# A one-input copy in place of a product with ones on GpSimd, in a hybrid attention step on one core

## The chip, the cores and the metric

The kernel runs on one NeuronCore of a Trainium2 chip. The metric is the device time of one execution in microseconds. A NeuronCore has a matrix engine (TensorE, PE in the profile; PEld is its weight load), VectorE (DVE), ScalarE (ACT), GpSimd (POOL) and SyncE (SP), which here only issues DMAs. They run their own instruction lists and wait for each other by semaphores.

## The reference

Two layers of a streaming encoder are applied to 1024 frames of a new stream and 64 frames of a running one; both share all weights. Everything is float32.

```python
# even layer: x -> x + y @ w_out
h = rmsnorm(x); z = h @ w_in                    # 1024 -> 5648 columns
aq, ak, av, bq, bk, bv, blr, gate = split(z)
ao = sliding_window_attention(aq, ak, av)       # 16 heads of 64, 4 KV heads, chunks of 64, sinks, ALiBi
bo = rmsnorm(gla(bq, bk, bv, log_sigmoid(blr @ w_lr + b_lr) / 16))   # 4 heads, 128 x 256 state
y = concat(ao, bo) * silu(gate)
# odd layer: x -> x + y @ w_out
xb, gate = split(rmsnorm(x) @ w_in)             # 1024 -> 2 x 1536
u = causal_conv4(xb)                            # width 4, per channel
rg, ig = sigmoid(blockdiag(u, w_ra)), sigmoid(blockdiag(u, w_ri))
a = exp(-8 rg softplus(-lam)); b = sqrt(1 - a*a) * ig * u
h_t = a_t * h_(t-1) + b_t                       # a scan over time
y = h * silu(gate)
# at the end: rmsnorm of x; keys, values and states are returned too
```

## The kernel before, in words

Activations lie transposed in the on-chip memory, features on the 128 partitions and 1092 columns of time, taken in 3 chunks of 364. Every weight matrix is cut into pieces of 128 x 1024 numbers, 113 of them, in the order in which they are used. A float32 product is made of three matmuls in the shorter format float32r: the weight W is split into w_hi (W rounded to float32r) and w_lo = W - w_hi, the activation likewise into H_hi and H_lo, and PE adds w_hi*H_hi + w_lo*H_hi + w_hi*H_lo.

The weight's path has four engines. SP loads piece p into `raw[:, p % 2]`, once `w_split` says that both halves of piece p - 2 are split (L326). GpSimd splits it in two halves of 512 columns: `w_hi` (L349), then `w_lo` (L353), in the slot p % 2 of each. Before it overwrites a half of `w_hi` it waits until PE is through with that half of the piece two before (`half_done` for the first half, `piece_done` for the second, L348). PE waits for `w_split` before the first matmul that reads a half (L382, L427), so at any time one piece is being multiplied and the next is split. SP's and GpSimd's loops run over pairs of pieces; the first two pieces, which wait for nothing of PE's, and the last one stand outside GpSimd's loop.

The stages, by the trace's time: the norm of x and the first pieces (0 to about 60 us); keys and values; attention (about 104 to 485 us), in which the matmuls of the next group of heads (L562) lie between scores (L494), transposes (L510) and products with the values (L522); the gated linear attention, four heads (to about 840); its output projection and the second layer's norm (to about 1050); the second layer's four groups (to about 1440); its output projection and the final norm.

VectorE's instructions that the prediction speaks of: L1171 makes H_lo at the start, L1236 copies a group's last values before attention starts on it, L1296 scales the probabilities, L1594 and L1598 are the first and the three further steps of the convolution, L1605 the low part of u, L1611 to L1616 the input term of the scan, L1619 and L1621 the scan for both streams, L1624 takes the gate's projection out of PSUM, which lets PE have that PSUM set again, and L1570 makes the low part of y. In the second layer's groups these run one behind the other on one engine for each of three 128-channel blocks, and PE waits for `drained`, `u_lo_done` or `y_lo_done` when it has no other work left. `ones` is a 128 x 128 tile of ones, also used by PE to sum over partitions.

Of the kernel before, what the change touches and what calls it, by code (L numbers as in the profile page):

```python
# [26 lines left out]
ALU = mybir.AluOpType  # L27
# [4 lines left out]
P = 128  # L32
# [29 lines left out]
PIECES = PC_OO + 2 * KD + 1  # L62
HALF = PIECE // 2
# [59 lines left out]
def tail_cols(c):  # L123
    a, b = TAIL[c]
    return slice(a * P, min(b * P, LIVE))
# [15 lines left out]
def build_program(nc, xT, weights, vecs_d, consts_d, wlr_d, kc_d, vc_d, sg_d,  # L141
# [5 lines left out]
    with ctx:  # L147
        at_byte = [32 * -(-nc.sbuf_base // 32)]

        def sb(name, shape, dt=F32, at=None):  # L150

            size = 4 * int(np.prod(shape[1:]))
            if at is None:
                at = at_byte[0]
                at_byte[0] += 32 * -(-size // 32)
            return nc.alloc_sbuf_tensor_at(name, shape, dt, offset=at)

        def sem(name):
            return ctx.enter_context(nc.semaphore(name))
# [7 lines left out]
        raw = sb("raw", [P, 2, PIECE])  # L167
        w_hi = sb("w_hi", [P, 2, PIECE], F32R)
# [3 lines left out]
        ones = sb("ones", [P, P])[:, :]  # L172
# [104 lines left out]
        ones_set, w_hi_done, w_split = sem("ones_set"), sem("w_hi_done"), sem("w_split")  # L277
# [40 lines left out]
        @block.sync  # L318
        def _(sp):
            sp.dma_start(raw[:, 0, :], weights[0]).then_inc(w_in[0], 16)  # L320
            sp.dma_start(X[:, 0, :], xT[0]).then_inc(x_in[0], 16)
            sp.dma_start(raw[:, 1, :], weights[1]).then_inc(w_in[1], 16)
            with sp.Fori(1, PIECES // 2 - 2) as i:
                for s in range(2):
                    sp.wait_ge(w_split, 4 * i + 2 * (s - 1))
                    sp.dma_start(raw[:, s, :], one(weights, 2 * i + s)).then_inc(w_in[s], 16)  # L326
            for piece in range(PIECES - 4, PIECES - 1):
                sp.wait_ge(w_split, 2 * piece - 2)
                sp.dma_start(raw[:, piece % 2, :], weights[last_pieces(piece)]).then_inc(w_in[piece % 2], 16)
            for c in range(3):  # L330
                cols = tail_cols(c)
                for b0, b1 in ((0, TAIL_POOL), (TAIL_POOL, 6), (6, KD)):
                    if b0:
                        sp.wait_ge(xn_done, (KD - TAIL_POOL) * c + b1 - TAIL_POOL)
                    else:
                        sp.wait_ge(xp_done, TAIL_POOL * (c + 1))
                    sp.dma_start(yT[b0:b1, :, cols].rearrange("b p n -> p b n"), X[:, b0:b1, cols])\
                      .then_inc(y_saved, 16)


        @block.gpsimd
        def _(pool):
            def split(i, s, first):
                pool.wait_ge(w_in[s], 16 * i + 16)
                for h in range(2):
                    cols = slice(h * HALF, (h + 1) * HALF)
                    if not first:
                        pool.wait_ge((half_done, piece_done)[h], 2 * i + (s - 1))  # L348
                    pool.tensor_tensor(w_hi[:, s, cols].rearrange("p (k n) -> p k n", n=P),  # L349
                                       raw[:, s, cols].rearrange("p (k n) -> p k n", n=P), every_tile_ones,  # L350
                                       ALU.mult).then_inc(w_hi_done, 1)
                    pool.wait_ge(w_hi_done, 4 * i + (2 * s + h + 1))
                    pool.tensor_tensor(w_lo[:, s, cols], raw[:, s, cols], w_hi[:, s, cols].bitcast(F32),  # L353
                                       ALU.subtract).then_inc(w_split, 1)

            every_tile_ones = ones.rearrange("p (k n) -> p k n", k=1).to_broadcast([P, HALF // P, P])
            pool.memset(ones, 1.0).then_inc(ones_set, 1)
            pool.wait_ge(ones_set, 1)
            for s in range(2):
                split(0, s, True)  # L360
            with pool.Fori(1, PIECES // 2 - 1) as i:
                for s in range(2):
                    split(i, s, False)
            split(PIECES // 2 - 1, 0, False)
            for c in range(3):
                cols = tail_cols(c)
                for b in range(TAIL_POOL):
                    if c == 0:
                        pool.wait_ge(weighted, b + 1)
                    if b == 0:  # L370
                        pool.wait_ge(fb_done, c + 1)
                    pool.tensor_tensor(X[:, b, cols], X[:, b, cols], fb[:, cols], ALU.mult).then_inc(xp_done, 1)
# [3 lines left out]
        def _(pe):  # L376
# [127 lines left out]
            def transposes(u, U):  # L504
                t, _ = unit(u)
                pe.wait_ge(pt_free, U + 1)
                pe.wait_ge(p_done, U + 1)
                for kt, _, rows in key_tiles(t):
                    for j in range(2):
                        mm = pe.transpose(ps[0:rows, 5 + u % 2, (2 * kt + j) * P:(2 * kt + j + 1) * P],  # L510
                                          Ssb[:, u % 3, j, kt * P:kt * P + rows], ident)
                mm.then_inc(pt_done, 1)
# [1304 lines left out]
```

## Time and profile before

| | |
|---|---|
| median of 3 runs | 1598.69 us (1594.52 to 1599.26) |
| the profiled execution | 1598.26 us |
| its span, first to last instruction | 1596.2 us |
| mean granted clock of PE | 0.983 |
| busy: PE / DVE / ACT / POOL | 1523.5 / 927.8 / 456.1 / 689.6 us |
| POOL, products w_hi (L349) | 226, 333.1 us in sum |
| POOL, differences w_lo (L353) | 226, 349.5 us in sum |

The busy time of an engine is the sum of its instructions' times; an instruction that has started and is held up by another engine counts as busy, so a longer time can hold a wait. The granted clock is the share of TensorE's full clock of 2.4 GHz that it was given; 0.5 stands for 1.2 GHz. In the lists of waits, "PE ps L388 <- DVE Y L1624" reads: PE's matmuls of L388 sat idle until VectorE's instruction of L1624 had finished. Times in the order of time are microseconds from the span's start.

### The profile page before, as it was taken

To read this page: it belongs to the slowest core of one execution; us is meant where nothing else is said; L and a number is where in the kernel's file an instruction comes from. 1 tells how busy PE (TensorE), PEld (TensorE's weight loads), DVE (VectorE), ACT (ScalarE), POOL (GpSimd) and SP (SyncE) were. 2 spreads that over 40 slices of the span, in tenths; PEclk is the share of its full clock that TensorE was granted. 3 is DMA by queue.
4 is the path that set the end of the run, shared out by engine and by line. 5 is a ranking of instruction groups with operands and counts; after the bars stand their busy time and mean duration, and the time that the engine had idled before them with its cause. 6 is when DMAs were issued, how large, how long until landed. Compare 5 with 4: busy or idle time off the path is not lost.

```text
span 1596.2 us, 24860 instructions
## 1 busy us (share of the span) xinstructions
PE 1523.5 (95%) x9622; PEld 1432.1 (90%) x9622; DVE 927.8 (58%) x1423; ACT 456.1 (29%) x808; POOL 689.6 (43%) x466
## 2 busy tenths in 40 slices
PE   6998999999989999999999999989999999989997
PEld 5997777777769999999999999989999999989996
DVE  7114867777775454744459111378887878985113
ACT  5111423333353222122133000225335143362001
POOL 5252212222212333523435444556666565656553
PEclk9999999999999999999999999999999999999998
DMA  4210010100000111110112332111111111113223
GB/s 181 89 60 27 27 42 16 39 26 29 27 29 32 34 32 45 40 34 30 34 44 68 104 101 95 54 55 53 53 40 53 53 40 54 53 53 106 86 81 112
DMA packets 29330, 89.16 MB, mean 56 GB/s; under 512 B 3600, under 2 KB 8784, under 8 KB 29264
## 3 DMA queue, kind: packets, MB, share of 16 engines
q1 hardware_dynamic: 19632, 64.27, 12.1%
q10 hardware_dynamic: 9632, 23.91, 4.6%
q8 instruction: 53, 0.87, 0.2%
q14 instruction: 13, 0.11, 0.0%
HBM read 76.64 MB, written 11.67 MB: 55 GB/s over the span
## 4 chain that ended last, share of the span: by engine, by line
PE 56%; DVE 8%; issue 4%; POOL 2%; ACT 2%; ACTq 0%; POOLq 0%; DVEq 0%
PE ps L388 41%; PE ps L433 6%; POOL w_hi L349 1%; DVE Y L1598 1%; PE ps L707 1%; PE ps L562 1%; POOL w_lo L353 1%; PE ps L628 1%; PE ps L612 1%; PE ps L623 1%; DVE arena L1616 1%; DVE Yr L1383 1%; DVE arena L1613 1%; DVE arena L1621 1%; DVE arena L1619 1%
## 5 line engine op out<-in xcount | busy, mean ns | idle before, releaser
L349 POOL TENSOR_TENSOR w_hi<-raw,ones 128x512 fp32r<-128x512 f32 x226 | 333.1, 1474 | 864.1 <-PE ps L388 484.1
L388 PE MATMUL ps<-H,w_hi 128*128 128x364 f32 x2796 | 568.6, 331 | 23.3 <-DVE H L1171 15.2
L388 PEld LDWEIGHTS ps<-H,w_hi 128*128 128x128 f32 x2796 | 479.5, 189 | 27.0 <-issue 16.4
L388 PE MATMUL ps<-H,w_lo 128*128 128x364 f32 x1716 | 379.6, 330 | 0.0
L353 POOL TENSOR_TENSOR w_lo<-raw,w_hi 128x512 fp32r<-128x512 f32 x226 | 349.5, 1547 | 17.7
L388 PEld LDWEIGHTS ps<-H,w_lo 128*128 128x128 f32 x1716 | 300.2, 189 | 0.0
L562 PE MATMUL ps<-H,w_hi 128*128 128x364 f32 x672 | 148.0, 347 | 0.0
L388 PE MATMUL ps<-Yr,w_hi 128*128 128x364 f32 x636 | 140.7, 329 | 0.0
L907 ACT ACTIVATE arena<-arena,sm 128x256 f32<-128x256 f32 (+1 forms) x144 | 69.6, 484 | 225.3 <-DVE sm L1282 225.3
L433 PE MATMUL ps<-w_hi,H 128*128 128x256 f32 (+1 forms) x720 | 132.4, 284 | 1.6 <-POOL w_lo L353 1.0
L1520 DVE TENSOR_TENSOR arena<-ps,arena 128x1092 f32 (+1 forms) x15 | 19.4, 1295 | 195.3 <-PE ps L388 195.3
L562 PEld LDWEIGHTS ps<-H,w_hi 128*128 128x128 f32 x672 | 115.5, 194 | 11.2 <-issue 10.5
L433 PEld LDWEIGHTS ps<-w_hi,H 128*128 128x128 f32 (+1 forms) x720 | 110.0, 185 | 3.1 <-POOL w_lo L353 1.8
L388 PEld LDWEIGHTS ps<-Yr,w_hi 128*128 128x128 f32 x636 | 110.8, 189 | 0.0
L433 PE MATMUL ps<-w_lo,H 128*128 128x256 f32 (+1 forms) x360 | 101.5, 282 | 0.0
L1082 ACT ACTIVATE arena<-arena 128x1092 f32<-128x1092 f32 x15 | 16.8, 1118 | 258.7 <-DVE arena L1520 253.6
L1270 DVE SCALAR_TENSOR_TENSOR arena<-consts,cur_sink,ps 128x256 f32<-128x256 f32 (+1 forms) x144 | 59.4, 453 | 51.6 <-PE ps L494 50.6
L388 PE MATMUL ps<-ur,w_hi 128*128 128x364 f32 x336 | 72.1, 342 | 13.2 <-DVE Y L1624 8.3
L562 PE MATMUL ps<-H,w_lo 128*128 128x364 f32 x336 | 78.5, 343 | 0.0
L388 PEld LDWEIGHTS ps<-ur,w_hi 128*128 128x128 f32 x336 | 59.8, 197 | 15.7 <-DVE Y L1624 10.6
L433 PEld LDWEIGHTS ps<-w_lo,H 128*128 128x128 f32 (+1 forms) x360 | 66.5, 185 | 0.3
L1598 DVE SCALAR_TENSOR_TENSOR Y<-arena,cur,Y 128x1092 f32<-128x1092 f32 x36 | 65.9, 1830 | 1.3
(202 smaller groups left out, 1894.0 us busy)
## 6 DMA issues: line engine op xcount, KB each, us to landing
raw<-weights SPq DMA_DIRECT2D x113, 512.0 KB, 3.3
arena<-xT ACTq DMA_DIRECT2D x15, 546.0 KB, 5.0
x_scratch<-arena ACTq DMA_DIRECT2D x8, 546.0 KB, 5.3
arena<-x_scratch ACTq DMA_DIRECT2D x8, 546.0 KB, 3.6
arena<-k_scratch ACTq DMA_DIRECT2D x8, 304.0 KB, 4.3
yT<-arena SPq DMA_DIRECT2D x2, 768.0 KB, 4.4
yT<-arena SPq DMA_DIRECT2D x2, 576.0 KB, 3.3
k_scratch<-Y ACTq DMA_DIRECT2D x2, 512.0 KB, 2.7
```

Of the source, the lines that this page charges most:

```text
L349: pool.tensor_tensor(w_hi[:, s, cols].rearrange("p (k n) -> p k n", n=P), raw[:, s, cols].rearrange("p (k n) -> p k n", n=P), every_tile_ones,
L353: pool.tensor_tensor(w_lo[:, s, cols], raw[:, s, cols], w_hi[:, s, cols].bitcast(F32), ALU.subtract).then_inc(w_split, 1)
L388: mm = pe.matmul(sets[st][:, c, 0:CW], lw[:, s, w], rx[:, k, c * CW:(c + 1) * CW], start=(first and n == 0 and m == 0), stop=(last and n = ...
L433: mm = pe.matmul(ps[0:m, 6 + t % 2, 0:256], lx[:, k, t * P:t * P + m], rw[:, s, wk], start=(k == 0 and n == 0), stop=(k == KD - 1 and n == 2))
L562: mm = pe.matmul(sets[0][:, c, 0:CW], lw[:, 1 - n % 2, k * P:(k + 1) * P], rx[:, k, c * CW:(c + 1) * CW], start=(x == 0), stop=(x == 3 * K ...
L612: pe.matmul(ps[:, 6 + t % 2, 0:256], kdT[0:r, t % 2, :], Vb[0:r, t, :], start=True, stop=True).then_inc(gds_done, 1)
L623: pe.matmul(ps[:, 3 + t % 2, e * P:e * P + r], Vb[0:r, t, cols], aT[0:r, t % 2, 0:r], start=True, stop=False)
L907: act.activation(Ssb[0:r, r3, j, c0:c1], Ssb[0:r, r3, j, c0:c1], ACT.Exp, bias=sm[0:r, r3, 2 + j:3 + j], scale=float(A_DIM) ** -0.5, accum ...
L1082: act.activation(sq, X[:, b, :], ACT.Square).then_inc(sq_done, 1)
L1270: last = dve.scalar_tensor_tensor(Ssb[0:r, r3, j, c0:c1], dist[0:r, c0:c1], cur_sink[0:r, 2, 2 * b + j:2 * b + j + 1], ps[0:r, 3 + j, c0:c ...
L1520: dve.tensor_tensor(chunks(slot(X, 2 * i + s)), setv(s), chunks(res[:, s, :]), ALU.add)\
L1598: dve.scalar_tensor_tensor(U[:, n, :], xc[:, j:j + TOK], cur[:, n, j:j + 1], U[:, n, :], ALU.mult, ALU.add).then_inc(cv_step if j < 3 else ...
```

## The change

Two things are changed in GpSimd's program. The high part is made by a copy from `raw` to `w_hi`, which converts float32 to float32r, in place of a product of `raw` with the tile of ones repeated along the free dimension. And the loop over pairs of pieces is written out, so that every wait compares with a constant; the waits themselves, their counts and the order of the pieces stay.

```diff
-                    pool.tensor_tensor(w_hi[:, s, cols].rearrange("p (k n) -> p k n", n=P),
-                                       raw[:, s, cols].rearrange("p (k n) -> p k n", n=P), every_tile_ones,
-                                       ALU.mult).then_inc(w_hi_done, 1)
+                    pool.tensor_copy(w_hi[:, s, cols], raw[:, s, cols]).then_inc(w_hi_done, 1)
                     pool.wait_ge(w_hi_done, 4 * i + (2 * s + h + 1))
                     pool.tensor_tensor(w_lo[:, s, cols], raw[:, s, cols], w_hi[:, s, cols].bitcast(F32),
                                        ALU.subtract).then_inc(w_split, 1)
 
-            every_tile_ones = ones.rearrange("p (k n) -> p k n", k=1).to_broadcast([P, HALF // P, P])
+
             pool.memset(ones, 1.0).then_inc(ones_set, 1)
             pool.wait_ge(ones_set, 1)
-            for s in range(2):
-                split(0, s, True)
-            with pool.Fori(1, PIECES // 2 - 1) as i:
-                for s in range(2):
-                    split(i, s, False)
-            split(PIECES // 2 - 1, 0, False)
+            for piece in range(PIECES - 1):
+                split(piece // 2, piece % 2, piece < 2)
```

On GpSimd, at the start of its program, before (ISA is an instruction without operands that the profile shows; here it is the pool's configuration, MODIFY_POOL_CONFIG):

```order
L357 MEMSET ones 128x128
L349 ISA
L349 TENSOR_TENSOR w_hi<-raw,ones 128x512 [waits w_in0,ones_set]
L353 TENSOR_TENSOR w_lo<-raw,w_hi 128x512 [waits w_hi_done]
L349 TENSOR_TENSOR w_hi<-raw,ones 128x512
L353 TENSOR_TENSOR w_lo<-raw,w_hi 128x512 [waits w_hi_done]
```

and the same place now, where w_lo's line has become L351:

```order
L355 MEMSET ones 128x128
L349 CAST w_hi<-raw 128x512 [waits w_in0,ones_set]
L351 ISA
L351 TENSOR_TENSOR w_lo<-raw,w_hi 128x512 [waits w_hi_done]
L349 CAST w_hi<-raw 128x512
L351 TENSOR_TENSOR w_lo<-raw,w_hi 128x512 [waits w_hi_done]
```

The configuration has moved from before the first operation on the weights to behind the first copy.

On GpSimd, the body of the loop before:

```order
L348 ISA [waits w_in0]
L349 TENSOR_TENSOR w_hi<-raw,ones 128x512 [waits half_done]
L352 ISA
L353 TENSOR_TENSOR w_lo<-raw,w_hi 128x512 [waits w_hi_done]
L349 TENSOR_TENSOR w_hi<-raw,ones 128x512 [waits piece_done]
L352 REGISTER_ALU
L353 TENSOR_TENSOR w_lo<-raw,w_hi 128x512 [waits w_hi_done]
L349 TENSOR_TENSOR w_hi<-raw,ones 128x512 [waits half_done,w_in1]
L352 REGISTER_ALU
L353 TENSOR_TENSOR w_lo<-raw,w_hi 128x512 [waits w_hi_done]
```

and the same pieces written out, which repeats to the end of the program:

```order
L349 CAST w_hi<-raw 128x512 [waits half_done,w_in0]
L351 TENSOR_TENSOR w_lo<-raw,w_hi 128x512 [waits w_hi_done]
L349 CAST w_hi<-raw 128x512 [waits piece_done]
L351 TENSOR_TENSOR w_lo<-raw,w_hi 128x512 [waits w_hi_done]
L349 CAST w_hi<-raw 128x512 [waits half_done,w_in1]
L351 TENSOR_TENSOR w_lo<-raw,w_hi 128x512 [waits w_hi_done]
```

The order of the operations on the weights is the same; the instructions that computed the counts to wait for are gone. GpSimd's program has 467 rows in place of 44. No other engine's instructions change.

## Rows read from the trace of the kernel before

**Rows 1.** The page, part 1: busy us (share of span) xinstructions.
```profile
PE 1523.5 (95%) x9622; PEld 1432.1 (90%) x9622; DVE 927.8 (58%) x1423; ACT 456.1 (29%) x808; POOL 689.6 (43%) x466
```

**Rows 2.** Stages: us, busy (x) per engine, granted clock, DMA, GB/s.
```profile
0.00:60.00 60.00, 44.81 (x244) 42.63 (x245) 32.26 (x26) 22.99 (x24) 29.84 (x24) 0.94 0.37 138
104.00:485.00 381.00, 355.78 (x2363) 290.57 (x2362) 264.58 (x780) 128.97 (x455) 87.86 (x68) 0.97 0.10 30
485.00:840.00 355.00, 352.43 (x2389) 336.54 (x2388) 183.74 (x234) 91.80 (x127) 129.00 (x88) 1.00 0.11 36
1050.00:1440.00 390.00, 372.14 (x2180) 367.90 (x2179) 321.39 (x278) 152.50 (x134) 237.97 (x140) 0.98 0.16 50
1194.00:1204.00 10.00, 7.61 (x37) 7.31 (x36) 7.24 (x8) 2.23 (x3) 4.85 (x4) 0.83 0.15 54
```

**Rows 3.** Waits of TensorE: engine line <- releaser: us, times, longest.
```profile
PE ps L388 <- DVE H L1171: 15.2, 4, 9.4
...
PE ps L510 <- DVE arena L1296: 11.0, 11, 1.7
...
PE ps L494 <- DVE arena L1236: 10.0, 4, 2.9
...
PE ps L388 <- DVE Y L1624: 8.3, 7, 2.4
...
PE ps L388 <- issue: 5.5, 2, 4.8
...
PE ps L388 <- DVE Yr L1570: 4.3, 1, 4.3
...
PE ps L433 <- POOL w_lo L353: 1.0, 4, 0.3
```

**Rows 4.** GpSimd's groups by form: busy us, mean ns | idle before.
```profile
L353 POOL TENSOR_TENSOR w_lo<-raw,w_hi 128x512 fp32r<-128x512 f32 x226 | 349.5, 1547 | 17.7
...
L349 POOL TENSOR_TENSOR w_hi<-raw,ones 128x512 fp32r<-128x512 f32 x226 | 333.1, 1474 | 864.1 <-PE ps L388 484.1 <-PE ps L562 254.6 <-PE ps L433 122.1
...
L372 POOL TENSOR_TENSOR arena<-arena 128x192 f32<-128x192 f32 x3 | 1.7, 590 | 1.8 <-ACT arena L1056 1.8
...
L357 POOL MEMSET ones<- 128x128 f32 x1 | 0.2, 205 | 0.3 <-POOLq L1800 0.3
...
L1800 POOL MEMSET const-float32-1.0<- 128x1 f32 x1 | 0.1, 99 | 0.0
```

**Rows 5.** By source line: duration ns min/median/max, first and last start.
```profile
L349 POOL TENSOR_TENSOR w_hi<-raw,ones x226: 1262/1295/2912, 4.3 to 1560.9; 128x512 fp32r<-128x512 f32 x113
...
L349 POOLq MODIFY_POOL_CONFIG  x2: 12/12/12, 0.9 to 0.9; - x2
...
L1594 DVE TENSOR_SCALAR Y<-arena,cur x12: 847/1764/1769, 1055.2 to 1369.4; 128x1092 f32<-128x1092 f32 x12
...
L1619 DVE TENSOR_TENSOR_SCAN arena<-arena x12: 2291/3266/3270, 1096.9 to 1425.7; 128x1024 f32<-128x1024 f32 x12
```

**Rows 6.** Order of time around 1175 to 1198 us: start us, us, what.
```profile
1175.96 1.38 POOL L349 TENSOR_TENSOR w_hi<-raw,ones 128x512 fp32r<-128x512 f32 x1 [0.36 <-PE ps L388]
...
1179.61 2.33 POOL L349 TENSOR_TENSOR w_hi<-raw,ones 128x512 fp32r<-128x512 f32 x1
...
1190.85 2.19 POOL L349 TENSOR_TENSOR w_hi<-raw,ones 128x512 fp32r<-128x512 f32 x1 [2.67 <-PE ps L388]
...
1176.23 6.88 DVE L1598 SCALAR_TENSOR_TENSOR Y<-arena,cur,Y 128x1092 f32<-128x1092 f32 x3
...
1191.92 3.27 DVE L1619 TENSOR_TENSOR_SCAN arena<-arena 128x1024 f32<-128x1024 f32 x1
...
1197.64 1.28 PE L388 MATMUL ps<-ur,w_hi 128*128 128x364 f32 x3 [2.39 <-DVE Y L1624]
```

**Rows 7.** Order of time, start of the program.
```profile
10.37 2.34 POOL L349 TENSOR_TENSOR w_hi<-raw,ones 128x512 fp32r<-128x512 f32 x1
...
11.50 2.37 DVE L1171 SCALAR_TENSOR_TENSOR H<-arena,vecs,H 128x1092 fp32r<-128x1092 f32 x1
```

## The prediction

> **What bounds the kernel now.** I read the page's busy shares first, then the stages, then who TensorE waits for, then GpSimd's own groups, and last the order of time at the places where TensorE stands still. TensorE is busy 1523.5 of 1596.2 us [rows 1]; the reader is to see that no other engine comes near, so only what fills or widens its 72.7 us of gaps can move the end, with what its clock loses around them. GpSimd, the engine that is changed, is busy 43% and sits idle 864.1 us in front of its high-part products, waiting for TensorE to free a weight slot [rows 1, 4]. Hence the change can't pay by GpSimd's throughput. The stages show where the gaps lie: 15.2 us in the first 60 us, 25.2 us in the attention stage (104 to 485), 2.6 us in the gated linear attention (485 to 840), 17.9 us in the second layer's groups (1050 to 1440) [rows 2]. The waits name their releasers: nearly all are VectorE instructions, and GpSimd itself is waited for in 1.0 us only [rows 3].
>
> So the question is what GpSimd does to VectorE. The rows of one instruction at its shortest and its median answer it: the bias of the convolution (L1594) takes 0.85 us at its shortest and 1.76 us in the median, the long scan (L1619) 2.29 and 3.27 us [rows 5]. In the order of time, each long one has a GpSimd operation running across its start: the scan begins at 1191.92 and a high-part product, issued at 1190.85, ends at 1193.04; the three convolution steps from 1176.23 to 1183.11 last 6.88 us while products run from 1175.96 and from 1179.61 [rows 6]. At the start of the program the product of 10.37 ends at 12.71, and VectorE's split of x, issued at 11.50, takes 2.37 us [rows 7]. The two engines take turns: a VectorE instruction that comes second is longer by about 0.9 to 1.0 us, and the GpSimd operation that comes second is longer too (1.26 us at its shortest, 1.47 in the mean, up to 2.91) [rows 4, 5].
>
> The Trainium skill says the same (SBUF — State Buffer, "Who interferes with whom"): the second port pair is one exclusive lock for the whole instruction, and whoever comes second blocks until the other ends. The trace agrees, with 2.29 against 3.27 us for the scan.
>
> **The change part by part.** *The copy.* It replaces 226 products that take 1.26 us undisturbed [rows 5]. No row shows a copy on GpSimd, so its time is bounded. Below: writing alone costs (205 - 99) ns over 127 elements, 0.83 ns each, plus 0.1 us [rows 4]; 512 elements give 0.53 us. On the other side of that: the two-input operation costs (1262 - 590) ns over 320 elements, 2.1 ns each [rows 4, 5], so a copy whose conversion costs as much as a second input is worth 1.26 us, and one that costs twice that slope besides 0.2 us is 2.4 us, the far end. I take 0.55 us, near the row of the writer with one stream, since the removed stream is the second read. The saving is then 0.7 us per operation.
>
> The Trainium skill (GPSIMD Engine Reference, "Engine selection") puts one-input operations at roughly line rate, by which the copy would be an estimated 0.5 to 0.6 us. The same page ("Elementwise — side-by-side cycle accounting") has 1.8 cycles per element as the best case of a tight loop, by which it would be an estimated 0.8 to 0.9 us and the sum below a little over half as large; no row here decides between the two.
>
> 226 times 0.7 us is 158 us of GpSimd's time, of which 864.1 us of idle [rows 4] hides all but what VectorE or TensorE waits for. I counted, in the order of time, the products that lie across VectorE's chain in front of a TensorE wait:
> - Start: two products, at 10.37 [rows 7] and 14.96, each between VectorE instructions that gate TensorE's first tiles: 2 x 0.7 = 1.4 us of the 15.2 [rows 3].
> - Attention: the four entries of a group wait 10.0 us for the small copies of L1236 [rows 3]; a product and then a difference precede them, and the copy before them bounds the gain to 0.5 us each: 2.0 us. Of the eleven waits on L1296, four or so have a product in the softmax's small steps, 0.6 us each: 2.4 us of 11.0.
> - Gated linear attention: the 1.0 us in which TensorE waits for the low parts [rows 3] goes: 1.0 us.
> - Second layer: four products before the wait of 4.8 us at 1072.7 (listed as issue), three before each of the two waits of 2.4 us (L1624), four before the one of 4.3 us (L1570) [rows 3, 6]: 14 x 0.7 = 9.8 us.
> - Clock: after the 2.39 us wait at 1197.64 [rows 6] the ten microseconds from 1194 have a granted clock of 0.83 [rows 2], so a third of them, 3.4 us, is at 1.2 GHz and costs 1.7 us. Where the wait shrinks to 0.3 us I expect no fall: two places, 3.4 us.
>
> Sum: 1.4 + 2.0 + 2.4 + 1.0 + 9.8 + 3.4 = 20.0 us. I take two thirds, 13 us, because the turns shift: a shorter copy lets the difference after it start earlier, at times across a VectorE instruction that was free before, and part of each chain belongs to ScalarE, which the change leaves alone.
>
> *The loop.* Written out, the program has no register or branch instructions between operations. On a chain of GpSimd this could only count if GpSimd were late; the next operation starts 0.1 us after the last in the looped part as well (1.38 us from 1175.96, the next at 1177.42). I cost it at nothing. If the fetch of some 460 instructions in place of 44 stalled, the 864.1 us of idle would cover it except in the 1.0 us of low-part waits.
>
> *The moved library instruction.* The pool configuration (0.9 us into the run, 12 ns by itself) stood before the first product, behind which GpSimd waited for the first weights anyway until 4.30 [rows 5]. Now it stands behind the first copy, so whatever it starts is in front of the first difference. That is 0 to 3.4 us (the length of the cover it had), and since TensorE's first wait lasts until 9.4 [rows 3] and the first low part would be ready at about 6.2 (4.30 + 0.55 + 1.26 and the step between them), the cover left is 3.2 us: nothing. Nor do SP's loads move; they wait for the same counts.
>
> The profiled execution took 1598.26 us (its span and 2.1 us around it), the median is 1598.69; the forecast is 1598.7 - 13, rounded to 1586 us.
>
> **The rivals.** *The copy is no shorter than the product* (1.2 to 1.4 us, or its conversion takes the time that the second read took). For it speaks that the cost per element of the product may be a software loop and not the port; against it the memset's 0.83 ns. Then nothing moves: 1597 to 1600 us.
>
> *The copy is shorter but VectorE's turns don't shorten*, because the difference, which comes right behind and is unchanged at 1.29 us, slides into the freed place. For it: between two VectorE instructions only one GpSimd operation fits, and there are as many as before. Against it: the products named above are separate turns. It leaves the 1.0 us of low-part waits and the start, 2 to 4 us: 1595 to 1597 us.
>
> *The copy is longer than the product*, and this is the slower case: a conversion loop that reads one stream but costs more per element. It decides from about 1.7 us on. The place is the same 28 turns (2 at the start, 8 in attention, 4 where the low parts are waited for, 14 in the second layer); at 2.4 us it adds 1.15 us to each, 32 us, by the same two thirds 21: 1620 us; at 1.8 us it is 10 us: 1609. Nothing in the trace excludes it, as no one-input arithmetic of this engine is in it; the memset speaks against it.
>
> *The copy at a middle price*, halfway between 0.53 and 1.26: 0.9 us saves 0.37 us a turn, so about half of 13: 1592 us. It belongs to the faster case, at its edge. The best-case loop of the page on GPSIMD in the Trainium skill (GPSIMD Engine Reference) would come out there.
>
> **How the numbers follow.** A measurement of this kernel tells about 0.3% (4.8 us) from no change. The copy at 0.5 to 1.0 us with its effect on the chains: 57%, 1578 to 1593 us, and 1586 as its value. Shorter but without effect: 10%. As long as the product: 13%. Longer: 20%. Faster by over 0.3% takes the first and a little of the second, 0.60; within 0.3% the rest of the middle ones, 0.18; slower 0.22, the last and a fetch or placement that goes wrong. The range runs from 1576 (the 20.0 us in full, and a little more clock) to 1609, where the copy of 1.8 us ends; about one in ten lies above it and somewhat less below.
>
> **What would show it.** The copy's row tells first: 0.5 to 0.9 us each is my case, over 1.5 us the slower one. Then the median of L1594 and L1619 should fall by 0.3 to 0.7 us, the waits on L1624 shrink from 2.4 to under 1 us and that on L1570 from 4.3 to about 2, the granted clock between 1194 and 1204 return to 1, and the waits for the low part vanish. VectorE's 927.8 us busy should fall by some 50 us. I am wrong if the copy is short and these waits stay, or if TensorE's first matmul moves behind 9.43 us.

## The result, and the profile after

The changed kernel takes 1561.36 us in the median (1556.69 to 1564.16, 4 runs) against 1598.97 us of the kernel before (1594.52 to 1600.82); the ratio is 0.9767, 95% interval [0.9745, 0.979]. It was timed once more beside other kernels: 1561.88 us against 1593.38, ratio 0.9793 [0.9766, 0.982]. So the gain is 2.1 to 2.3%, 31 to 38 us, where 13 were forecast; 1561 lies below the range of 1576 to 1609, and also below 1579, where the forecast's sum would have led without its discount.

The busy shares of the changed kernel, answering to [rows 1]; its span is 1554.8 us:

```profile
PE 1506.1 (97%) x9622; PEld 1419.1 (91%) x9622; DVE 850.3 (55%) x1423; ACT 455.9 (29%) x808; POOL 514.3 (33%) x466
```

TensorE is busy 17 us less for the same 9622 matmuls and idle 48.7 us in place of 72.7; VectorE is busy 77 us less with the same 1423 instructions.

Stage by stage, cut at the same matmuls in both traces: the start, attention, the gated linear attention, the second layer's groups. The columns are the stretch, its length, busy time (and instructions) of PE, PEld, DVE, ACT, POOL, then the granted clock, DMA share and GB/s. Before:

```profile
0.00:59.50 59.50, 44.31 (x240) 42.13 (x241) 32.00 (x25) 22.99 (x24) 29.62 (x23) 0.94 0.37 139
137.70:476.50 338.80, 316.45 (x2119) 251.54 (x2119) 252.62 (x760) 125.17 (x449) 72.41 (x56) 0.97 0.10 29
476.50:840.80 364.30, 360.94 (x2447) 345.05 (x2447) 190.10 (x248) 94.43 (x132) 129.66 (x88) 1.00 0.11 36
1045.10:1434.50 389.40, 371.68 (x2184) 367.57 (x2184) 318.74 (x277) 147.30 (x130) 240.95 (x142) 0.98 0.15 49
```

After:

```profile
0.00:56.40 56.40, 43.98 (x240) 42.31 (x241) 28.98 (x25) 23.12 (x24) 21.89 (x23) 0.97 0.38 147
134.20:459.60 325.40, 309.02 (x2118) 244.72 (x2118) 242.48 (x761) 125.09 (x449) 53.09 (x56) 0.99 0.09 31
459.60:818.80 359.20, 358.58 (x2446) 343.31 (x2446) 178.56 (x248) 94.12 (x131) 93.89 (x88) 1.00 0.10 36
1023.10:1392.50 369.40, 364.12 (x2185) 362.60 (x2184) 271.70 (x277) 146.47 (x129) 182.31 (x142) 1.00 0.15 52
```

The stages are shorter by 3.1, 13.4, 5.1 and 20.0 us. TensorE's idle time in them goes from 15.2 to 12.4, from 22.3 to 16.4, from 3.4 to 0.6 and from 17.7 to 5.3 us. What remains of the differences, in the attention stage more than half, is time in which TensorE was busy longer for the same matmuls: its clock. How much of the gain that is over all runs stands at the end of the experiments.

Who TensorE waits for, answering to [rows 3] (L382 was L388, L488 was L494, L504 was L510, L1564 was L1570):

```profile
PE ps L382 <- DVE H L1165: 12.4, 3, 9.3
PE ps L488 <- DVE arena L1230: 8.4, 4, 2.8
PE ps L504 <- DVE arena L1290: 6.7, 10, 1.6
PE ps L382 <- DVE Yr L1564: 3.6, 2, 3.4
PE ps L382 <- issue: 2.5, 2, 1.9
```

The waits on L1624 are gone altogether. They were three of 2.39 us and four of 0.2 to 0.3: besides the one that [rows 6] shows, at 1197.64, these two before:

```profile
1295.07 0.77 PE L388 MATMUL ps<-ur,w_hi 128*128 128x364 f32 x3 [2.39 <-DVE Y L1624]
1392.64 0.77 PE L388 MATMUL ps<-ur,w_hi 128*128 128x364 f32 x3 [2.39 <-DVE Y L1624]
```

A wait in the gated linear attention that [rows 3] leaves out is gone too:

```profile
PE ps L388 <- DVE arena L1436: 1.9, 1, 1.9
```

The wait for the low part of u (under issue) has shrunk from 4.8 us to 1.9, the waits for the softmax (L504) from 11.0 to 6.7, the one on the low part of y from 4.3 to 3.4. GpSimd's low parts are waited for in 0.2 us.

GpSimd's two groups, as in [rows 4]:

```profile
L351 POOL TENSOR_TENSOR w_lo<-raw,w_hi 128x512 fp32r<-128x512 f32 x226 | 324.9, 1437 | 18.1
L349 POOL CAST w_hi<-raw 128x512 fp32r<-128x512 f32 x226 | 182.0, 805 | 997.0 <-PE ps L382 605.2 <-PE ps L556 260.4 <-PE ps L427 126.8
```

and by source line, as in [rows 5]: the copy, the pool's configuration, the first convolution step, the long and the short scan:

```profile
L349 POOL CAST w_hi<-raw x226: 608/612/2494, 4.1 to 1519.6; 128x512 fp32r<-128x512 f32 x113
...
L351 POOLq MODIFY_POOL_CONFIG  x2: 11/11/11, 4.7 to 4.7; - x2
...
L1588 DVE TENSOR_SCALAR Y<-arena,cur x12: 847/849/918, 1033.2 to 1333.4; 128x1092 f32<-128x1092 f32 x12
...
L1613 DVE TENSOR_TENSOR_SCAN arena<-arena x12: 2291/3269/3273, 1070.0 to 1384.8; 128x1024 f32<-128x1024 f32 x12
...
L1615 DVE TENSOR_TENSOR_SCAN arena<-arena,cur x12: 320/634/771, 1072.2 to 1388.0; 128x64 f32<-128x64 f32 x12
```

The copy takes 0.61 us alone, and 0.81 in the mean, since it too waits. The differences, which nobody touched, fell from 1547 to 1437 ns. The convolution's first step fell to its shortest time in the median (1764 to 849 ns); the long scan did not in the median (3266 to 3269): eight of its twelve were long before, five behind a difference and three behind a product, and eight are long now, all behind a difference. The place below is one of the three that had a product before and are free now; three others, free before, now meet a difference. The configuration now stands at 4.7 us and takes 11 ns: the next difference starts at 4.80, 0.07 us behind the copy's end, and TensorE starts at 9.27, not later than before.

The same transition between two groups as in [rows 6], in order of time, start us, us, what:

```profile
1145.74 0.61 POOL L349 CAST w_hi<-raw 128x512 fp32r<-128x512 f32 x1 [2.94 <-PE ps L382]
...
1146.44 1.29 POOL L351 TENSOR_TENSOR w_lo<-raw,w_hi 128x512 fp32r<-128x512 f32 x1
...
1147.91 0.85 DVE L1588 TENSOR_SCALAR Y<-arena,cur 128x1092 f32<-128x1092 f32 x1
...
1163.68 2.49 POOL L349 CAST w_hi<-raw 128x512 fp32r<-128x512 f32 x1 [3.94 <-PE ps L382]
...
1163.47 2.29 DVE L1613 TENSOR_TENSOR_SCAN arena<-arena 128x1024 f32<-128x1024 f32 x1
...
1165.68 0.64 DVE L1615 TENSOR_TENSOR_SCAN arena<-arena,cur 128x64 f32<-128x64 f32 x1
```

Before, two rows of the same places that [rows 6] did not show, and the short scan:

```profile
1174.31 1.29 POOL L353 TENSOR_TENSOR w_lo<-raw,w_hi 128x512 fp32r<-128x512 f32 x1
...
1174.42 1.77 DVE L1594 TENSOR_SCALAR Y<-arena,cur 128x1092 f32<-128x1092 f32 x1
...
1195.11 1.28 DVE L1621 TENSOR_TENSOR_SCAN arena<-arena,cur 128x64 f32<-128x64 f32 x1
```

The reader is to see three things. The copy and the difference behind it start with TensorE's release (1145.74) and are over at 1147.73, before VectorE's convolution starts at 1147.91. Before, the difference began at 1174.31 and the convolution found it running (1.77 us in place of 0.85). That is not all gain: in the changed kernel the small copy of three columns in front of the convolution (L1584, L1590 before) finds the same difference and takes 0.83 us in place of 0.18, so that about 0.3 us are left of the 0.9. Second, the long scan takes 2.29 us in place of 3.27 because VectorE's chain, by then 1.3 us ahead, starts it at 1163.47, before TensorE releases GpSimd at 1163.68; before, the release came 1.07 us ahead of the scan. Third, a short instruction of VectorE takes as long as the GpSimd operation that it meets: the scan over 64 columns met a difference before (1.28 us) and meets a copy now (0.64 us), and it takes 0.32 us where it comes first. TensorE in the ten microseconds that answer to 1194 to 1204 of [rows 2]:

```profile
1163.00:1173.00 10.00, 10.00 (x62) 10.00 (x61) 8.69 (x9) 3.78 (x4) 6.56 (x5) 1.00 0.16 54
```

It does not wait, and the granted clock stays at 1.00.

### The profile page after: what moved, and what is told of

The parts are those of the page before. It is cut to its first block, busy times and chain, and to the rows that moved or that the text cites. A ratio compares the mean times of both kernels' runs of the same rounds, so it can differ in the third digit from the quotient of the medians.

```text
span 1554.8 us, 24474 instructions
## 1 busy us (share of the span) xinstructions
PE 1506.1 (97%) x9622; PEld 1419.1 (91%) x9622; DVE 850.3 (55%) x1423; ACT 455.9 (29%) x808; POOL 514.3 (33%) x466
## 4 chain that ended last, share of the span: by engine, by line
PE 71%; DVE 2%; issue 1%; ACT 0%; ACTq 0%; DVEq 0%
PE ps L382 54%; PE ps L427 7%; PE ps L701 1%; PE ps L556 1%; PE ps L622 1%; PE ps L606 1%; PE ps L617 1%; PE ps L596 1%; DVE Yr L1377 1%; PE ps L593 1%; PE ps L591 1%; PE ps L526 0%; PE ps L488 0%; PE ps L516 0%; PE ps L504 0%
## 5 line engine op out<-in xcount | busy, mean ns | idle before, releaser
L382 PE MATMUL ps<-H,w_hi 128*128 128x364 f32 x2796 | 567.9, 331 | 16.8 <-DVE H L1165 12.4
L349 POOL CAST w_hi<-raw 128x512 fp32r<-128x512 f32 x226 | 182.0, 805 | 997.0 <-PE ps L382 605.2
L382 PEld LDWEIGHTS ps<-H,w_hi 128*128 128x128 f32 x2796 | 479.6, 189 | 19.8 <-issue 14.6
L382 PE MATMUL ps<-H,w_lo 128*128 128x364 f32 x1716 | 379.5, 330 | 0.0
L351 POOL TENSOR_TENSOR w_lo<-raw,w_hi 128x512 fp32r<-128x512 f32 x226 | 324.9, 1437 | 18.1
L382 PEld LDWEIGHTS ps<-H,w_lo 128*128 128x128 f32 x1716 | 300.1, 189 | 0.0
L382 PE MATMUL ps<-Yr,w_hi 128*128 128x364 f32 x636 | 140.9, 330 | 0.0
L382 PEld LDWEIGHTS ps<-Yr,w_hi 128*128 128x128 f32 x636 | 110.8, 189 | 0.0
L382 PE MATMUL ps<-ur,w_hi 128*128 128x364 f32 x336 | 66.8, 328 | 1.9 <-issue 1.9
L556 PEld LDWEIGHTS ps<-H,w_lo 128*128 128x128 f32 x336 | 58.2, 189 | 1.5 <-issue 1.5
L382 PEld LDWEIGHTS ps<-ur,w_hi 128*128 128x128 f32 x336 | 57.0, 188 | 2.2 <-issue 2.2
```

Of the source, the lines that this page charges most:

```text
L349: pool.tensor_copy(w_hi[:, s, cols], raw[:, s, cols]).then_inc(w_hi_done, 1)
L382: mm = pe.matmul(sets[st][:, c, 0:CW], lw[:, s, w], rx[:, k, c * CW:(c + 1) * CW], start=(first and n == 0 and m == 0), stop=(last and n = ...
L556: mm = pe.matmul(sets[0][:, c, 0:CW], lw[:, 1 - n % 2, k * P:(k + 1) * P], rx[:, k, c * CW:(c + 1) * CW], start=(x == 0), stop=(x == 3 * K ...
```

## The experiments

Twelve runs told apart where the gain comes from. The first theory (A) is that GpSimd's operations hold VectorE up less. In its simple form the sum of GpSimd's reading time decides; once that had fallen, two forms stood against each other: the parts of the weights come earlier (A1), or the length of the single operation that a VectorE instruction meets decides (A2). The rival is the program written out without its loop. "Half-speed time" is the part of the whole span in which TensorE was granted 1.2 GHz: twice the span times one minus the mean granted clock.

**The program written out, with the product.**

```diff
-            for s in range(2):
-                split(0, s, True)
-            with pool.Fori(1, PIECES // 2 - 1) as i: ...
+            for piece in range(PIECES - 1):
+                split(piece // 2, piece % 2, piece < 2)
```

> The program written out, but with the product in place of the copy. If the turns at the shared port are all of it (theory A: a shorter GpSimd operation holds VectorE up for less), this is the kernel before: 1597 to 1601 us, TensorE's idle time about 73 us, L1594's median 1.76 us. If the missing loop (no counts computed between operations) is part of the gain (theory B), it lies clearly below 1594 us.

Measured: 1594.08 us against 1597.92, ratio 0.9985 [0.9964, 1.0005]: no difference that can be told. TensorE's idle time is 70.7 us. The missing loop is not the gain; the copy is (1594.08 to 1561, the rest of the change). The interval leaves room for up to 6 us; the table at the end, which takes the clock out, for about 1.

**A spare copy behind each difference, and a spare memset there.** The first gives GpSimd back the reading time that the change took away, the second only busy time. Both write a spare tile of 512 numbers in bfloat16, which nobody reads, and both begin with the third piece, so the start of the kernel is as in the changed one. (The edits shown leave out two lines: the one that makes the tile, and one wait, before the first spare operation, for the constants to be loaded.)

```diff
                                        ALU.subtract).then_inc(w_split, 1)
+                    if not first:
+                        pool.tensor_copy(spare[:, :], consts[:, 0:512])
```

> The changed kernel with a spare copy of 512 columns behind each difference, 222 in all; it reads a constant table and nobody uses what it writes. It gives GpSimd back about 0.6 us per half piece of reading. By theory A most of the gain is lost again: 1585 to 1600 us, TensorE's idle time 60 to 75 us, and the half-speed time of its clock back to 30 us or more. By theory B, and by a theory C that only the time until w_lo is ready counts (the spare copy comes after it and there are 997 us of idle), it stays at 1561 to 1566 us.

```diff
+                        pool.memset(spare[:, :], 0.0)
```

> As the spare copy, with a memset of the same 512 columns in its place, about 0.53 us: GpSimd is as busy but reads nothing. If the shared read port is what VectorE waits for (theory A), VectorE's operations with two inputs are not held up, only the one-input ones that write through both ports (L1594): 1561 to 1570 us. If any GpSimd operation holds VectorE up, it comes out within 5 us of the spare copy.

Measured: 1567.1 us with the spare copy (ratio 0.9808 [0.9765, 0.9851]) and 1566.17 with the memset (0.9806 [0.9764, 0.9848]). Both return 5 to 6 us of the 37, so the sum of GpSimd's reading time, back at its old size with the copy (712 us for the weights, 683 before), does not make the kernel before: the simple form of theory A had said 1585 us at the least and missed by 18. The two medians lie within 5 us of each other, which had been expected if any GpSimd operation holds VectorE up, and within 1561 to 1570, which had been expected if only reads do; by themselves they decide nothing. In the second layer's groups alone the two differ. The spare copy:

```profile
1030.90:1405.20 374.30, 365.75 (x2185) 363.34 (x2184) 280.33 (x277) 147.72 (x131) 270.15 (x213) 1.00 0.16 51
```

the spare memset:

```profile
1033.10:1402.80 369.70, 364.43 (x2185) 362.92 (x2185) 273.37 (x277) 146.93 (x130) 213.98 (x213) 1.00 0.16 52
```

The stage takes 374.3 us with the copy and 369.7 with the memset, against 369.4 in the changed kernel: there the memset costs 0.3 us and the copy 4.9. In attention both stages are longer (332.6 and 333.6 against 325.4), of which 1.3 and 2.2 us are idle time and 5.9 and 6.0 the clock; another run of the changed kernel (below) has 328.4 there, so only part of that is the spare operation's. Over the whole kernel and all runs, with the clock taken out (table at the end), the copy costs 5.5 us and the memset 2.2: a write is cheaper, but not free everywhere.

**The spare operations ahead of the high part.**

```diff
+                    if not first:
+                        pool.tensor_copy(spare[:, :], consts[:, 0:512])
                     pool.tensor_copy(w_hi[:, s, cols], raw[:, s, cols]).then_inc(w_hi_done, 1)
```

> The spare copy of the constant table stands ahead of each high part in place of behind each difference; its result is used by nobody. Theory A1 (what counts is which VectorE instruction finds a GpSimd read under way, and the first 1.3 us behind TensorE's release are free because VectorE reads PSUM then): w_hi and w_lo come 0.6 us later, as with the product, and most of the gain goes: 1580 to 1592 us. Theory A2 (only the length of one uninterrupted GpSimd operation counts, a turn of 0.6 us being cheap): it stays near the spare copy behind, 1565 to 1570 us.

> A memset of 512 columns ahead of each high part: GpSimd's operations come 0.5 us later but read no more than in the changed kernel. If lateness against VectorE's chain is what the product cost (a part of A1), it takes back half of the gain or more, 1575 to 1590 us; if only the port's reading time counts, it stays at 1562 to 1568 us.

Measured: 1565.92 us with the copy (0.9812 [0.9788, 0.9836]) and 1562.35 with the memset (0.9785 [0.9761, 0.9809]). High and low parts come 0.5 to 0.6 us later, and it costs 1 to 4.6 us. A1 had said 1575 us at the least for both. That GpSimd is late against VectorE is thus not what the product cost; what is left is A2: two operations of 0.6 us one behind the other, in the place of one of 1.3 us, do not hold VectorE up as that one did.

**The product in two parts.** The test of A2 without any copy:

```diff
-                    pool.tensor_tensor(w_hi[:, s, cols]..., raw[:, s, cols]..., every_tile_ones, ALU.mult)
+                    for q in range(2):
+                        part = slice(h * HALF + q * HALF // 2, h * HALF + (q + 1) * HALF // 2)
+                        mul = pool.tensor_tensor(w_hi[:, s, part]..., raw[:, s, part]..., every_tile_ones[:, 0:2, :], ALU.mult)
+                    mul.then_inc(w_hi_done, 1)
```

> No copy at all: the written-out program with the product, but each product in two operations of 256 columns, about 0.7 us each, so GpSimd reads 0.15 us longer per half piece than before the change. If the length of one operation is what VectorE waits for (A2), most of the gain comes without the copy: 1562 to 1578 us. If GpSimd's reading time in sum counts, it is no faster than before, 1595 to 1605 us.

Measured: 1580.29 us against 1593.38, ratio 0.991 [0.9875, 0.9945]; 13 us below the kernel before (14 below the written-out product of the other session, 1594.08), though GpSimd does more:

```profile
L351 POOL TENSOR_TENSOR w_hi<-raw,ones 128x256 fp32r<-128x256 f32 x452 | 421.6, 954 | 772.1 <-PE ps L388 403.4 <-PE ps L562 244.2 <-PE ps L433 120.3
L356 POOL TENSOR_TENSOR w_lo<-raw,w_hi 128x512 fp32r<-128x512 f32 x226 | 335.4, 1484 | 17.7
```

That is 757 us of busy time where the kernel before had 683, and the kernel is faster: the length of a single operation counts, and not the sum. But it ends 2 us above the band that A2 had been given, and 18 us above the copy: it wins back only about a third of the gain. Two operations of 0.7 us are more than one of 0.6, and other than the spare operations they also run in the first two pieces; TensorE's waits for H at the start are 16.2 us here and 12.9 with the spare copy ahead. That these two things are the whole of the 18 us is argued, not shown.

**The differences in two and in four parts**, with the copy as it is:

```diff
-                    pool.tensor_tensor(w_lo[:, s, cols], raw[:, s, cols], w_hi[:, s, cols].bitcast(F32), ALU.subtract)
+                    for q in range(2):      # four in the other kernel
+                        part = slice(h * HALF + q * HALF // 2, h * HALF + (q + 1) * HALF // 2)
+                        sub = pool.tensor_tensor(w_lo[:, s, part], raw[:, s, part], w_hi[:, s, part].bitcast(F32), ALU.subtract)
+                    sub.then_inc(w_split, 1)
```

> The changed kernel with each difference in two operations of 256 columns, about 0.7 us each: GpSimd reads 0.15 us longer in all, but no operation of it holds the port for more than 0.7 us. If the length of a turn counts (A2), VectorE gains once more: 1545 to 1557 us. If the sum of the reading time or the number of turns counts, it is the same or slower: 1560 to 1572 us.

> The changed kernel with each difference in four operations of 128 columns, about 0.44 us each by the slope of 2.1 ns (1.8 us in sum in place of 1.29). By A2 a turn gets shorter still, but GpSimd takes part in more turns: 1550 to 1560 us. If the growing sum counts, 1560 to 1575 us.

> The changed kernel with each difference in two parts, once more, beside the changed kernel itself: 3 to 6 us below it, 1553 to 1559 us.

> The changed kernel once more, on the same chip as the kernel with differences in two parts: 1558 to 1564 us by the runs so far. Its number of stretches at half clock is expected to differ from the first profile's (three before the end), by up to two, as the fixed parts of other runs do.

Measured: two parts 1556.2 us (0.9749 [0.972, 0.9777]) and again 1556.59 (0.9769 [0.9742, 0.9795]); four parts 1552.7 (0.9742 [0.9715, 0.977]); the changed kernel beside the last two 1561.88 (0.9793 [0.9766, 0.982]), six runs each. The four parts' runs (1551.09 to 1556.55) and those of the two parts (1555.72 to 1558.83) lie below all six runs that the changed kernel had beside them (1558.93 to 1563.86), though its earliest runs reached 1556.69. So the kernel with four parts beats the changed kernel by 9 us and the kernel before by 41 us; about 3 of the 9 us are there with the clock taken out, and the rest is the clock (table at the end). It has 904 operations of 0.61 us in the mean:

```profile
L353 POOL TENSOR_TENSOR w_lo<-raw,w_hi 128x128 fp32r<-128x128 f32 x904 | 523.6, 610 | 18.1
```

Its sum is 523.6 us where the changed kernel spends 324.9 on the differences. The short scan tells in each kernel how long the GpSimd operation is that it meets. Its rows (ns, min/median/max) in the kernel before, with the spare copy ahead, with the product in two parts, and with the differences in four:

```profile
L1621 DVE TENSOR_TENSOR_SCAN arena<-arena,cur x12: 1283/1304/1317, 1099.1 to 1428.9; 128x64 f32<-128x64 f32 x12
```

```profile
L1621 DVE TENSOR_TENSOR_SCAN arena<-arena,cur x12: 627/1312/1315, 1078.0 to 1394.9; 128x64 f32<-128x64 f32 x12
```

```profile
L1621 DVE TENSOR_TENSOR_SCAN arena<-arena,cur x12: 746/758/1311, 1088.5 to 1409.8; 128x64 f32<-128x64 f32 x12
```

```profile
L1618 DVE TENSOR_TENSOR_SCAN arena<-arena,cur x12: 480/482/486, 1068.5 to 1384.5; 128x64 f32<-128x64 f32 x12
```

It takes 0.32 us where it comes first. Behind an operation that had been waiting for the long scan to end it is longer by about 0.3 us less than that operation lasts: by 1.0 us for 1.3, 0.44 for 0.7, 0.31 for 0.6, 0.16 for 0.44. (Where the two start at once it is somewhat more, 0.77 us in all beside a copy in the changed kernel.) The long scan says the same, 2.29 us where it comes first; with the spare copy ahead and with the differences in four:

```profile
L1619 DVE TENSOR_TENSOR_SCAN arena<-arena x12: 2578/2581/3270, 1074.9 to 1392.4; 128x1024 f32<-128x1024 f32 x12
```

```profile
L1616 DVE TENSOR_TENSOR_SCAN arena<-arena x12: 2432/2440/2441, 1066.2 to 1382.1; 128x1024 f32<-128x1024 f32 x12
```

That is 0.29 us more behind a copy and 0.15 behind a quarter of a difference, against 0.98 behind a product or a whole difference.

The chain in front of L1624, from VectorE's first read of PSUM (L1586) to L1624's end, at the transition of [rows 6], follows the lengths of GpSimd's operations; TensorE has work for about 22.3 us of it (24.71 before, less the wait of 2.39):

| kernel | GpSimd's operations per half piece | chain, us |
|---|---|---|
| before | 1.3 + 1.3 | 24.71 |
| product in two parts | 0.7 + 0.7 + 1.3 | 23.78 |
| spare copy behind | 0.6 + 1.3 + 0.6 | 23.30 |
| spare copy ahead | 0.6 + 0.6 + 1.3 | 22.63 |
| spare memset ahead | memset + 0.6 + 1.3 | 22.28 |
| changed, and with spare memset behind | 0.6 + 1.3 | 21.79 |
| differences in two parts | 0.6 + 0.7 + 0.7 | 21.36 |
| differences in four parts | 0.6 + 4 x 0.44 | 20.24 |

In these rows each of VectorE's instructions waits for one GpSimd operation at most, and their number is fixed; more and shorter ones only make GpSimd later, and it has 997.0 us of idle time in front of the copies to be late in. The table also explains why the loss is not in proportion: below 22.3 us a longer chain costs nothing at this place, and above it every tenth counts. TensorE's wait behind it is 1.47 us with the product in two parts, 0.99 with the spare copy behind, 0.32 with it ahead, and none in the changed kernel.

**The product in one stage alone.**

```diff
+                    if PC_A + 2 <= 2 * i + s < PC_B0 + 2:      # in the other: PC_C + 2 <= ... < PC_OO + 2
+                        pool.tensor_tensor(w_hi..., raw..., every_tile_ones, ALU.mult).then_inc(w_hi_done, 1)
+                    else:
                         pool.tensor_copy(w_hi[:, s, cols], raw[:, s, cols]).then_inc(w_hi_done, 1)
```

> The changed kernel with the product for the pieces that are split during the attention stage alone (about 40 products). The traces give this stage 13.4 us of the gain, 5.9 us of idle time and 8.5 us from 17 us less at half clock. If the stages' shares add up, 1572 to 1578 us, with most of the half-speed time of this stage (20.5 us before, 3.4 after) back; if the clock's falls are chance and not tied to the products, about 1567 us.

> The changed kernel with the product for the pieces of the second layer's groups alone (72 products). The traces give this stage 20.0 us of the gain, 12.4 us of idle time and 5.9 us from the clock. If the shares add up: 1578 to 1584 us, and the waits on L1624 of about 2.4 us and on u_lo of 4.8 us are back, with the other stages as after the change.

Measured: attention, with 32 products (about 40 had been expected), 1569.27 us (0.9815 [0.9769, 0.9861]); the groups, with 72, 1581.69 (0.9913 [0.9888, 0.9938]). The groups' stage is the one of the kernel before again, 389.2 us where that took 389.4, and its waits are those of [rows 3]:

```profile
1028.00:1417.20 389.20, 371.43 (x2183) 367.35 (x2183) 317.55 (x277) 147.43 (x130) 239.57 (x142) 0.98 0.15 49
```

```profile
PE ps L388 <- DVE Y L1624: 8.3, 7, 2.4
...
PE ps L388 <- issue: 5.4, 2, 4.8
...
PE ps L388 <- DVE Yr L1570: 4.3, 1, 4.3
```

The shares, against 1561.4: 7.9 us attention, 20.3 us the groups; 9 of the 37 are left for the start, the linear attention and what varies. The groups fell into their band; for attention 1572 to 1578 us had been expected if the first trace's 13.4 us were the product's, and about 1567 if the clock's falls were chance: it came out between the two. The stage with the product there:

```profile
133.20:474.10 340.90, 319.27 (x2118) 253.40 (x2118) 251.93 (x761) 125.12 (x449) 69.23 (x56) 0.96 0.09 29
```

It has 21.6 us of idle time and 27.3 us at half speed.

**How much of it is the clock.** The second profile of the changed kernel has the same stages but for the clock, attention and groups:

```profile
134.40:462.80 328.40, 312.06 (x2118) 246.93 (x2118) 242.54 (x761) 125.17 (x449) 53.23 (x56) 0.98 0.10 30
...
1029.30:1398.70 369.40, 364.12 (x2185) 362.60 (x2183) 271.60 (x277) 146.59 (x129) 182.41 (x142) 1.00 0.16 52
```

Its idle time is 48.2 us (48.7 in the first profile), its span 1561.2 (1554.8), its mean granted clock 0.988 (0.994), that is 36 us at half speed in place of 19. So 17 us of half-speed time, 9 us of the kernel's, differ between two executions of the same program. The kernel before has 54 us, the written-out product 52, the product in attention 36 and in the groups 42. The clock's share of the gain is then (54 - 19) / 2 = 18 us by one profile and (54 - 36) / 2 = 9 us by the other.

The span and the granted clock of every run settle which. Span times mean granted clock is the time that a run would have taken with its half-speed time at full speed (a little too short where a half-speed stretch holds a wait). Means over all runs, us:

| kernel | runs | span | half-speed time | span x clock |
|---|---|---|---|---|
| before | 31 | 1593.9 | 48 | 1569.8 |
| product, written out | 10 | 1592.9 | 48 | 1569.1 |
| product in two parts | 4 | 1577.9 | 33 | 1561.4 |
| product in the groups | 4 | 1580.2 | 43 | 1558.9 |
| product in attention | 4 | 1566.2 | 30 | 1551.4 |
| spare copy behind | 4 | 1564.9 | 30 | 1550.1 |
| spare copy ahead | 4 | 1564.3 | 29 | 1549.8 |
| spare memset behind | 4 | 1564.0 | 34 | 1546.8 |
| spare memset ahead | 4 | 1560.3 | 30 | 1545.1 |
| changed | 10 | 1559.4 | 30 | 1544.6 |
| differences in two parts | 10 | 1554.7 | 23 | 1543.1 |
| differences in four parts | 6 | 1551.4 | 20 | 1541.3 |

The last column varies little: one run of a kernel differs from another by 1 to 2 us as a rule, where half-speed time ranges from 29 to 64 us before and from 19 to 37 in the changed kernel. So of 34.4 us of gain 25.2 are waits that went, as both profiles' idle time says (24.0 and 24.5), and 9.3 are the clock; the first profile, with 19 us at half speed, was the changed kernel's best run in that and not a typical one.

## Why the prediction was wrong

**What bounds the kernel, and the mechanism: right.** TensorE's gaps behind VectorE's chains, and VectorE held up by GpSimd's operations, are where the time came from. Putting the product back in one stage alone restored that stage's waits, in the groups to 0.1 us and in attention all but 0.6 us of 21.0. By the Trainium skill (SBUF — State Buffer, "Who interferes with whom") a VectorE instruction with two inputs in the on-chip memory contends with a GpSimd operation that reads that memory, and not with one that only writes. In the groups this case agrees: the spare copy cost 4.9 us and the memset 0.3.

**The copy's price: right.** 0.61 us, taken as 0.55, between the ends 0.53 and 1.26. The Trainium skill's line rate for one-input operations (GPSIMD Engine Reference, "Engine selection") agrees with it; the best-case loop of 1.8 cycles per element ("Elementwise — side-by-side cycle accounting"), by which an estimated 0.8 to 0.9 us was given, doesn't.

**The discount to two thirds: wrong, and with the wrong sign.** This step took 6.7 of 20.0 us away because the turns shift and the difference slides into the freed place. The idle time alone fell by 24.0 us, where the sum without clock and without discount was 16.6. The sliding did happen: three long scans that came first before now stand behind a difference, and the copy of three columns in front of the convolution is 0.65 us longer. But the chain as a whole gained more than the products' 0.7 us each. At 1172.9 three products should have shortened it by 2.1 us, and it shortened by 2.9: 1.2 in the three convolution steps, 1.0 because the long scan now starts before GpSimd is released, 0.65 because the short scan meets a copy, 0.3 at the convolution's start, less 0.2 at L1611 (L1605 now).

**The waits: some left out, one priced too high.** By stages, forecast and measured: start 1.4 and 2.8, attention 4.4 and 5.9, linear attention 1.0 and 2.7, groups 9.8 and 12.4. In the groups the prediction priced two waits of 2.4 us on L1624 where the trace of the kernel before has three, at 1197.64, 1295.07 and 1392.64, and all three went. In the linear attention it left out the wait of 1.9 us on L1436. The wait on L1570 was priced at 2.8 us and gave 0.9.

**The clock: mis-sized.** I priced 3.4 us for two places; over all runs it was 9 us. I had counted only waits that vanish from the groups, and none in attention, where the half-speed time was 20.5 us before and 3.4 and 10.2 us in the two profiles after, though the waits there shrank by 6 us only. I can't name a rule from these runs for which wait is followed by a fall. Of the three equal waits of 2.39 us before, two have a fall behind them (granted clock 0.83 in the ten microseconds from 1194, 0.87 from 1289) and the third has none (1.00 from 1386). That part stays open, as does whether a fall could be avoided by filling a wait with other matmuls, which wasn't tried.

So of some 21 us by which the forecast fell short of the mean gain, about 7 are the discount, 8 to 9 the waits and 6 the clock. That the change would pay at all, and through which engine, was no luck; the size was wrong in three terms, all three too low.

**The rivals.** A copy no shorter, or longer: out by its row. Turns that don't shorten, because the difference slides in: seen at three long scans, but out as an account of the whole. The loop: costed at nothing, and the written-out product confirms it within 6 us. The configuration behind the first copy: nothing, as costed.

**The expected signs.** The waits on L1624 fell to nothing (under 1 us said), that on L1570 only to 3.4 (about 2 said), L1594's median by 0.9 (0.3 to 0.7 said), the long scan's median not at all, VectorE's busy time by 77 us (50 said). The granted clock at the place that answers to 1194 to 1204 returned to 1 as said, and the waits for the low part shrank to 0.2 us where they should have vanished.

## What to carry to other kernels

Where GpSimd and VectorE both read the on-chip memory, look at how long one GpSimd operation is, and not only at how much it does: each VectorE instruction in the chain can wait for one of them. If GpSimd has slack, cut its operations into short ones, even where the sum grows; here four quarter-size differences in place of one cost 199 us more of GpSimd's time and gave 9 us of the kernel's, 3 of them without the clock. When waits of the matrix engine shrink, price its clock from all stretches at half speed in the trace, since here it was worth over a third as much as the waits; and take it from many runs, because it differs between executions: span times mean granted clock is far steadier than the time itself.

## What the runs showed of the hardware

- A one-input copy with conversion of 128x512 float32 takes 0.61 us on GpSimd, the two-input product or difference 1.26 us, a memset of 128x512 bfloat16 0.53.
- A short VectorE instruction takes the length of the GpSimd operation in whose turn it falls: the scan over 64 columns took 0.32 us where it met none, 0.63 behind a copy of 0.61, 1.28 behind a difference of 1.29 and 0.48 behind one of 0.44. Behind an operation that had been waiting, the surplus is its length less about 0.3 us, so in these rows four quarters of a difference would cost VectorE less (4 x 0.16 us) than the whole one (1.0), even if it met all four.
- Two executions of one program differed by 17 us in TensorE's time at 1.2 GHz, with waits that agreed to 0.5 us in sum; over 31 runs of the kernel before that time ranged from 29 to 64 us, while span times granted clock stayed within 1567 to 1574.
